# The order of turn, scores and value products in an attention loop on one Trainium2 core

## What is computed

```python
def one_block(qi):
    s = jnp.einsum('bqkgd,bskd->bkgqs', qi, k).astype(jnp.float32) * scale
    p = jax.nn.softmax(s, axis=-1).astype(v.dtype)
    return jnp.einsum('bkgqs,bskd->bqkgd', p, v)
```

## Time and profile before

| | |
|---|---|
| median of 3 runs | 2218.52 us (2217.17 to 2219.79) |
| the profiled execution's own time | 2220.07 us |
| its span, first to last instruction | 2218.2 us |
| mean granted TensorE clock | 0.989 of full speed |
| PE busy | 2137.0 us (96%) |
| DVE, ACT busy | 1455.2 us (66%), 890.6 us (40%) |
| attention loop of layer 0 | 161.30 to 217.64 us |
| of layer 2 | 1366.37 to 1447.72 us |
| of layer 3 | 1945.76 to 1982.65 us |

### The profile page before, as it was taken

How to read it: one execution, slowest core, us unless ns; L and a number is a source line. 1 busy time by engine, 2 the same in 40 slices (tenths; PEclk the granted TensorE clock), 3 DMA queues, 4 the chain that set the end, 5 groups by cost and what they waited for, 6 DMA issues and landing times.

```text
span 2218.2 us, 28535 instructions
## 1 busy us (share of the span) xinstructions
PE 2137.0 (96%) x11576; PEld 1747.4 (79%) x11576; DVE 1455.2 (66%) x2187; ACT 890.6 (40%) x1345; POOL 228.4 (10%) x253
## 2 busy tenths in 40 slices
PE   6999999999999998999999998999999999998998
PEld 4767888888787766988888796588888878868986
DVE  2426557878756686567878656856778775656554
ACT  3336443332244431533331254844333223455543
POOL 0000011110010036011110001101111100100110
PEclk9999999999999999999999999999999999999999
DMA  9650335546542211245546531023455553214554
GB/s 307 199 173 20 114 105 162 171 152 218 181 139 95 86 57 58 77 133 161 168 155 212 196 99 65 8 80 105 161 162 167 193 192 125 96 49 146 172 189 142
DMA packets 224680, 304.44 MB, mean 137 GB/s; under 512 B 6738, under 2 KB 153243, under 8 KB 224422
## 3 DMA queue, kind: packets, MB, share of 16 engines
q1 hardware_dynamic: 220541, 290.11, 39.7%
q0 software_dynamic: 3600, 12.35, 1.7%
q10 hardware_dynamic: 409, 0.16, 0.0%
HBM read 301.48 MB, written 1.11 MB: 136 GB/s over the span
## 4 chain that ended last, share of the span: by engine, by line
PE 81%; DVE 9%; ACT 4%; DMA 3%; POOL 1%; issue 1%; SPq 0%; ACTq 0%; DVEq 0%; POOLq 0%
PE lo L654 16%; PE lo L655 16%; PE lo L656 16%; PE lo L720 4%; PE lo L721 4%; PE lo L722 4%; PE hi L720 2%; PE hi L722 2%; PE hi L721 2%; DVE w_lo L1510 2%; PE lo L951 2%; ACT w_hi L1148 2%; DMA w_raw<-in_ffn_w_down 1%; PE lo L971 1%; PE stat L720 1%
## 5 line engine op out<-in xcount | busy, mean ns | idle before, releaser
L654 PE MATMUL lo<-u_hi,w_hi 128*128 128x512 f32 (+1 forms) x2016 | 717.1, 356 | 6.4 <-DVE w_lo L1510 4.5
L655 PE MATMUL lo<-u_lo,w_hi 128*128 128x512 f32 (+1 forms) x2016 | 704.8, 350 | 0.0
L656 PE MATMUL lo<-u_hi,w_lo 128*128 128x512 f32 (+1 forms) x2016 | 704.4, 349 | 0.0
L1510 DVE TENSOR_TENSOR w_lo<-w_raw,w_hi 128x2048 fp32r<-128x2048 f32 (+1 forms) x182 | 408.2, 2243 | 340.2 <-ACT w_hi L1148 338.8
L1148 ACT ACTIVATE w_hi<-w_raw 128x2048 fp32r<-128x2048 f32 (+1 forms) x182 | 339.8, 1868 | 478.5 <-DMA w_raw<-in_ffn_w_down 258.5
L654 PEld LDWEIGHTS lo<-u_hi,w_hi 128*128 128x128 f32 x2016 | 382.0, 189 | 71.1 <-issue 17.0
L656 PEld LDWEIGHTS lo<-u_hi,w_lo 128*128 128x128 f32 x2016 | 382.0, 189 | 49.8
L655 PEld LDWEIGHTS lo<-u_lo,w_hi 128*128 128x128 f32 x2016 | 382.3, 190 | 48.6 <-issue 0.7
L1527 DVE SCALAR_TENSOR_TENSOR mod_acc<-mod_raw,silu_c,mod_acc 128x512 f32<-128x512 f32 x504 | 394.4, 849 | 6.3 <-DMA mod_raw<-in_mod_w 6.2
L2072 POOL TENSOR_TENSOR mid_lo<-conv,mid_hi 128x512 fp32r<-128x512 f32 (+1 forms) x88 | 117.7, 1358 | 1057.8 <-ACT mid_hi L1489 1057.8
L720 PE MATMUL lo<-w_hi,mid_hi 128*128 128x512 f32 x374 | 147.6, 395 | 3.3 <-DVE u_raw L1601 2.5
(11 more groups left out here) (361 smaller groups left out, 2753.9 us busy)
## 6 DMA issues: line engine op xcount, KB each, us to landing
w_raw<-in_ffn_w_up SPq DMA_DIRECT2D x88, 1024.0 KB, 5.0
mod_raw<-in_mod_w SPq DMA_DIRECT2D x144, 512.0 KB, 3.9
w_raw<-in_ffn_w_down SPq DMA_DIRECT2D x40, 1024.0 KB, 5.0
mod_unit<-in_mod_w SPq DMA_DIRECT2D x24, 1024.0 KB, 6.4
w_raw<-in_a_w_qkv SPq DMA_DIRECT2D x12, 1024.0 KB, 5.6
w_raw<-in_b_w_in SPq DMA_DIRECT2D x12, 1024.0 KB, 5.1
w_raw<-in_a_w_out SPq DMA_DIRECT2D x8, 1024.0 KB, 5.1
w_raw<-in_ffn_w_down SPq DMA_DIRECT2D x8, 512.0 KB, 3.6
```

Source lines behind the costliest of these rows:

```text
L654: mm(o, h3[:, k, c], x, start=(first and k == 0), stop=False)
L655: mm(o, h3[:, k, c], y, start=False, stop=False)
L656: ins = mm(o, l3[:, k, c], x, start=False, stop=(last and k == nr - 1))
L1510: tt(WL[:, n % 3, 0:words], RAW[:, n % 3, 0:words], WH[:, n % 3, 0:words].bitcast(F32), ALU.subtract).then_inc(lo_ready, 1)
```

## The change

In each step of the loop, `pv` is called ahead of `turn` and `scores` and no longer behind them. Nothing else is touched: the same instructions with the same waits, on PE's queue alone, in another order.

```diff
                 for s in range(NH[i] // W):
+                    if s >= 2:
+                        pv(*pieces[s - 2])
                     for x in range(W * s, W * s + W):
                         turn(x)
                     while issued < min(NH[i], W * (s + 1) + 4):
                         scores(i, range(issued, issued + W))
                         issued += W
-                    if s >= 2:
-                        pv(*pieces[s - 2])
                 pv(*pieces[-2])
                 pv(*pieces[-1])
```

## The result

| | before | after |
|---|---|---|
| median of 16 runs each, on the same chip | 2217.39 us | 2223.69 us |
| profiled execution, its own time | 2220.07 us | 2220.98 us |
| layer 0's loop (granted clock) | 56.34 (0.95) | 56.25 (0.98) |
| layer 2's loop | 81.35 (0.98) | 85.20 (1.00) |
| layer 3's loop | 36.89 (0.95) | 38.66 (1.00) |

The ratio is 1.0028, with a 95% interval of 1.0021 to 1.0035: slower by 6.3 us (4.7 to 7.8). Forecast were 6.3 us and 2224.8 us.

A forecast was written before the change was run, and what follows sets the result against it. PE was taken as the bound, VectorE and ScalarE close behind. Terms 3.9 + 0.9 + 0.3 + 0.4 + 1.4 + 0.4 = 7.3 us were cut to 6.3, giving 2224.8 us; range 2220.5 to 2229.0.

The forecast's parts named there:

- Layer 2's groups: Layer 2, groups 2 to 6: each group's first value product waits 0.92 us for its copy, net 0.79, together 3.9 us.
- Layer 2's start: Layer 2's first steps: the first product waits for its copy, delaying turns and weight split, 0.9 us; P(1,0)'s wait 0.3 us.
- the branch that I had at about even chances: Layer 2's start: PE stays at 2.4 GHz, giving back 1.6 us while a wait grows to about 1; 0.9 us less in sum.
- End: Layer 2's end: P(7,0) waits 2.0 us for its copy, but the loop ends only 0.4 us later.
- Layer 3: Layer 3's loop: first product delays T(2) by 1.75 us, partly caught up, then a wait at the end; 1.4 us in all.
- Layer 0: Layer 0's loop: early delay partly made up by gapless PE work, a late copy holds the last group; 0.4 us.
- that for groups: Layer 2: five groups at full net price are the upper half of their 1.5 to 4.6 us, a reason to go below 7.3.
- Chains come earlier: Layer 2 mainly: earlier output copies let VectorE and ScalarE catch up, halving the waits; 3.5 us, 2222.0; 22 in 100.
- Clock falls at a new wait: Ends of layers 2 and 3: PE drops to the lower clock after new waits, 3.2 us more, 2228.0; 15 in 100.
- Product fills VectorE's wait: Waits for normalisation in layers 2 and 3: moved products fill PE's idle time, at most 6.9 us faster, 2211.6; 5 in 100.
- Weight loads: At PE's new stalls: if loads were pulled ahead past a waiting product, stalls cost nothing extra; otherwise 0.06 each, 0.7 us together.
- B: Theory from the experiments, not forecast: spacing sets the price; without a product between scores and next turn, turns wait for a normalisation.

The follow-up runs named there:

- run 9: Changed order with the weight split also moved to the loop's end, against the kernel before: 2217.01 us, ratio 0.9997.
- run 1: Kernel before with only pieces 1 and 2 of each group moved ahead of the turn, piece 0 left behind the scores: 2223.36 us beside 2217.88.

## Why the prediction was right

**The reading.** PE was the bound, and its operands, not its idle time, decided: V(15) ended 0.15 us ahead of P(2,0) in the trace after as computed from the trace before, and the wait of 0.92 measured 1392.17 - (1390.19 + 1.06) = 0.92 on PE, of which the row shows 0.85 as idle.

**Layer 2's groups**: 0.79 each, 3.9 us in all. Measured 0.69, and from T(10) to T(44), a stretch with five such waits, 58.67 against 55.22 us: 3.45. The wait was right; what comes back was mis-sized. I gave the turns behind it 0.13, from the modelled durations 1.29 and 1.16. From start to start the pair takes 1394.21 - 1393.18 = 1.03 behind the wait and took 1.22 there before: 0.19, and 0.02 more at the next pair.

**Layer 2's start**: T(8), the first turn behind the weight split, came 0.82 late (0.9 said). From there to T(10) the loop won 0.72 back. I had 0.3 lost with the slow clock and 0.6 won without it, and the clock was full, so the branch that I had at about even chances is the one that came in the two profiled executions. **End**: 0.30 (0.4 said). Together 3.85, where the full-clock case gave 4.6 and the other 5.5; the loop came to 85.2 us, not to about 87.

**Layer 3**: T(2) 1.84 late (1.75 said), T(4) 1.08 (0.9), T(15) 1.83 (1.4), loop +1.77 (1.4). That VectorE catches up to 0.5 before the end was wrong: the shift of T(13) was still 1.06. No term had this loop's clock, which rose from 0.95 to 1.00: from T(4) to T(5) PE took 3.68 us before and 3.02 after, in spite of 0.64 of waiting there. **Layer 0**: 0.09 shorter in one pair of executions, 0.31 longer in the other (0.4 said).

**The sum.** The loops grew by 5.5 and 5.8 us against 7.3 summed and 6.3 taken, and the time by 6.3. The point forecast is better than its terms deserve: the deduction for the clock held in the two executions profiled, that for groups was right in sign, layer 3's came out on the other side. The mechanism was right; that 6.3 was forecast and 6.3 measured to the tenth is luck, with an interval of 4.7 to 7.8 around the measurement and a clock that is worth about 2 us of it.

**The rivals.** *Chains come earlier*: refused, the wait stayed at its whole length. *Clock falls at a new wait*: not in either profiled execution of the changed kernel, where 1.91 us at layer 2's end went by at full clock. But its mechanism exists: in run 9 the same wait was followed by the lower level, at 1.5 us, near the 1.6 that the rival had for one fall. The changed kernel's 16 executions have granted clocks of 0.991 to 0.995, and its six at 0.991 and 0.992 took 2224.66 to 2226.78 us, the four at 0.995 2220.93 to 2223.43; where their clock fell is not on record. *Product fills VectorE's wait*: waits for line 1775 fell from 4.1 to 2.6 and from 2.8 to 1.2 us, but as a by-product of PE being late, and far less than the new waits of 7.8 and 4.4. **Weight loads.** The trace shows the load of the waiting product at 1392.14, 0.03 ahead of the product and 0.12 behind the end of the copy. What it loads are values, a tile of `v_tok` that had long been ready; the late operand is the other one, `probs_t`. Even so nothing was pulled ahead of the wait. "TensorE: Matmul & The Clock Gate", "Step-by-step: what each phase is for", in the Trainium skill, has loads pulled ahead of matmuls in flight. Here no matmul was in flight, and the load stands in PE's queue behind the same wait as the product; this trace shows no load pulled past it. The 0.06 behind each wait are inside the start-to-start figures.

**What I had not seen** is B. I took the price for that of P(g,0) alone, so I would have recommended to move only the other pieces; in that kernel, run 1, layer 2's loop grew by 3.3 us as against 3.85.

## What to carry to other kernels

Before work is moved forward in an engine's in-order queue, look up when the producer of its operand ends, not how long the engine idles there: a waiting instruction stops all behind it, and its place may also have been the filler between two dependent operations of the others. Where an engine waits, ask first what stands ahead of the late producer in its own queue and can go elsewhere; here one weight split moved to the loop's end gave 9 us, where every reordering of PE tried lost time or gave none. And before a difference of a few us is given to a mechanism, compare the granted clocks of the executions: here 0.001 of it over the span went with about 1.2 us.

## What the hardware showed unexpectedly

In layer 2 the clock rose where waits were added. Before, two waits of 0.82 and 0.75 us ahead of step 4's two turns are followed by a stretch at the lower level, 1.2 GHz, in both executions profiled. PE's timeline of the kernel before:

```profile
1380.07 0.66 PE L951 MATMUL lo<-ident,probs 128*128 128x128 f32 x4 [0.82 <-DVE probs L1775]
1381.47 0.66 PE L951 MATMUL lo<-ident,probs 128*128 128x128 f32 x4 [0.75 <-DVE probs L1775]
1382.06 1.79 PE L927 MATMUL hi<-k_dup,qkv 64*128 64x512 f32 x4
```

The same place after:

```profile
1377.81 0.66 PE L951 MATMUL lo<-ident,probs 128*128 128x128 f32 x4 [0.92 <-DVE probs L1775]
1379.21 0.66 PE L951 MATMUL lo<-ident,probs 128*128 128x128 f32 x4 [0.75 <-DVE probs L1775]
1379.80 1.13 PE L927 MATMUL hi<-k_dup,qkv 64*128 64x512 f32 x4
1381.69 1.08 PE L975 MATMUL lo<-probs_t,v_tok 128*64 128x256 f32 x8 [0.76 <-ACT probs_t L1369]
1382.70 1.09 PE L951 MATMUL lo<-ident,probs 128*128 128x128 f32 x8
```

The four scores take 1.13 us where they took 1.79, behind two waits of 1.67 together where there were 1.57, and a third wait changes nothing either. In the profiled executions this repeats: granted clocks of 1.00 in layers 2 and 3 in both after, 0.98 and 0.95 in both before. In layer 2 it is worth the 1.5 us that I had worked out from the earlier trace rows as 1.6, and there it paid for part of the new waits. The timed executions need not all follow: over the whole span their granted clocks overlap (0.989 to 0.994 before, 0.991 to 0.995 after). Which difference between the histories spares the clock was not found. That the length of the wait just before doesn't decide it is shown: 1.57 us in two pieces were followed by the lower level where 1.67 and one more wait were not, and 1.91 us were followed by it in run 9 and by full clock in both executions of the changed kernel.
